# Low parts of 14 weight tiles subtracted on GpSimd, last taps behind q and k, and a reordered head in a one-layer hybrid decoder kernel

## The chip, the cores and the metric

The kernel is one program on one core of a Trainium2 chip. The metric is the device time in microseconds of one execution, as the median of several; less is better. The engines are TensorE (PE, with its weight loads PEld), VectorE (DVE), ScalarE (ACT), GpSimd (POOL) and SyncE (SP, which here only issues DMAs). They run in parallel, each takes its own instructions strictly in program order, and they wait for each other by semaphores.

## The reference

One decoder layer for a sequence of 256 tokens, width 1024, all in float32:

```python
mod = silu(c) @ ada_w + ada_b                      # six vectors of 1024: shift, scale, gate, twice
xn = rmsnorm(x, norm1_g) * (1 + sc1) + sh1
q, k, v, ca, cg = split(xn @ w_in)                 # 5 x 512 columns
y_attn = attention(rmsnorm(q), rmsnorm(k), v)      # 8 heads of 64, causal, with a relative bias table
a = causal_dwconv(ca * sigmoid(cg))                # 31 taps, 512 channels
a = silu(group_norm(a))
x = x + g1 * (concat(y_attn, a) @ w_out)
xn2 = rmsnorm(x, norm2_g) * (1 + sc2) + sh2
u, g = split(causal_dwconv(xn2 @ w_up))            # 3 taps, 2 x 2816 channels
x = x + g2 * ((silu(g) * u) @ w_down)
```

With 256 tokens the attention has one block, so it is plain causal attention.

## The kernel before

**Tiles and the two parts of a number.** All weights arrive as 71 tiles of 128 partitions x 2048 float32 (1 MB each), in the order of the list `STREAM`: 24 `ada` tiles (the modulation), 4 `conv` tiles (the a and gate columns of the convolution), 4 `qk`, 2 `v`, 4 `out`, then `up` and `down` tiles of the feed-forward part in turn. SP issues one DMA per tile into a ring of 6 slots (`RAW`, tile `raw`). It issues tile n only when the tile 6 places ahead has been given up: an ada tile by PE (`ada_used`), another by the engine that subtracts its low part (`lo_done`). `SPLIT` numbers the tiles that aren't ada: conv 0 to 3, qk 4 to 7, v 8 and 9, out 10 to 13, up0 14, up1 15.

A product in nearly full float32 precision is made of three fast ones (`product`, L853 to L855): hi times hi, lo times hi, hi times lo. For each such tile, ACT copies the raw tile to `w_hi` (L336, `split_hi`), rounded, and DVE subtracts that from the raw tile into `w_lo` (L543, `split_lo`). There are 3 buffers (`PARTS`) for each, so tile m waits until PE has used tile m-3 (`w_used`). Activations are split in the same way (`act_hi`, `act_lo`).

**The head.** x arrives transposed in `xt`. ACT squares it (L342), PE sums the squares over partitions with a matrix of ones (L898), ACT takes the root, DVE the reciprocal (`rinv`, L549). For each of 8 tiles k of 128 channels: PE multiplies ada tile k with silu(c) (`ada_rows`, L909), ACT copies the rows (L348), PE turns them into columns (`ada_columns`, L923), DVE makes scale and shift (L565 to L569) and the modulated tile (L593, L596), ACT makes `act_hi` (L363), GpSimd (k under 5, L304) or DVE (L558) makes `act_lo`, and PE multiplies with the first two conv tiles (`first_products`). `PRODUCTS_AFTER` and `HIGH_AFTER` say after which ada tile PE and ACT do which k.

**The middle.** PE works through conv2, conv3 and the four qk tiles (some 7 us each with the ada tile behind it), then v in four halves (`v_half`), the rms of q and k (`qk_turn`, `qk_spread` L1018). DVE meanwhile does the depthwise convolution: 124 `taps` of 128x256 (62 for each of two pairs of channel tiles, L621; they accumulate in PSUM), one L543 for each weight tile, and q's and k's normalisation (`qk_normalise`, L675). In its order, 98 taps come before the reciprocal for q and k (L679), and all remaining 26 before `qk_normalise`.

**Attention, heads 0 to 7.** PE makes the scores (L1096), DVE adds the bias and takes the maximum (`add_bias`, L700), ACT the exponentials (L416), DVE divides (`normalise`, two L713 of 128x128 and 128x256), PE turns the probabilities (`head_turn`, L1106) and multiplies with v (L1116). Between heads PE does remaining ada tiles and the first six of eight parts of the output projection (`out_part`). DVE also makes the group norm's split parts (`mix_parts`, L663 and L666) at head 5, ACT copies the highs of out0 to out3 and up0 behind heads 0, 2, 4, 5, 6 (`HIGH_AT_HEAD`), DVE subtracts their lows behind heads 1, 4, 5, 6, 7 (`LOW_AT_HEAD`). GpSimd squares for the group norm (L309).

**Second norm.** DVE scales the projection by the gate (L767), GpSimd and DVE add the residual (L315, L775), DVE and ACT sum the squares (L777), PE transposes back (L1201), ACT, DVE and GpSimd make the parts of the second activations (L493, L783, L786, L319). The feed-forward part follows: 11 rounds of two up tiles and one down tile.

## Time and profile before

| | |
|---|---|
| median of 3 runs | 377.09 us (376.81 to 379.04) |
| the profiled execution's own time | 377.13 us, of which span 375.3 us |
| PE busy | 352.0 us (94%) |
| DVE busy | 267.4 us (71%) |
| ACT busy | 176.9 us (47%) |
| POOL busy | 23.9 us (6%) |
| DMA | 79.51 MB, mean 212 GB/s |
| mean granted TensorE clock | 0.986 |

"Busy" is the union of an engine's instruction times. All times below are in microseconds from the start of the span; the span begins with the first instruction and ends with the last.

### The profile page before, as it was taken

How to read it: one execution, taken by the hardware profiler on the slowest of the kernel's cores; microseconds unless marked ns; L12 is line 12 of the kernel's file. 1: busy time of each engine (PE TensorE's matmuls, PEld its weight loads, DVE VectorE, ACT ScalarE, POOL GpSimd, SP SyncE). 2: the span in 40 equal slices, each digit the busy share in tenths (PEclk: the TensorE clock that was granted, in tenths of full speed). 3: DMA queues.
4: the chain of work that ended last, by engine and by line, in shares of the span. 5: the costliest groups of instructions: out<-in, count | busy, mean ns of one | idle time of the engine just before them, and what ended most of it. 6: DMA issues, size and time to landing. Idle time of an engine off the chain costs nothing.

```text
span 375.3 us, 6080 instructions
## 1 busy us (share of the span) xinstructions
PE 352.0 (94%) x2408; PEld 295.6 (79%) x2408; DVE 267.4 (71%) x486; ACT 176.9 (47%) x251; POOL 23.9 (6%) x67
## 2 busy tenths in 40 slices
PE   1999899999499989999999999999999999999995
PEld 1677788897245437777799899998989899999984
DVE  0393799999996558756888776768586667658665
ACT  3442833352102465837674553635544644636430
POOL 7421000000000200002300000000000000000000
PEclk9999999999889899999999999999999999999999
DMA  8999958798774496551074544654635545510003
GB/s 317 428 422 417 366 209 329 260 344 346 312 289 160 152 371 261 203 199 47 2 283 167 220 148 194 221 165 176 223 123 217 186 160 215 176 50 2 3 0 113
DMA packets 12653, 79.51 MB, mean 212 GB/s; under 512 B 1352, under 2 KB 2768, under 8 KB 3280
## 3 DMA queue, kind: packets, MB, share of 16 engines
q1 hardware_dynamic: 12416, 78.97, 55.2%
q8 instruction: 19, 0.31, 0.3%
q10 hardware_dynamic: 144, 0.13, 0.1%
q14 instruction: 10, 0.08, 0.1%
q0 software_dynamic: 64, 0.01, 0.0%
HBM read 78.05 MB, written 1.06 MB: 211 GB/s over the span
## 4 chain that ended last, share of the span: by engine, by line
PE 80%; DVE 12%; ACT 3%; DMA 3%; issue 1%; POOL 0%; SPq 0%; DVEq 0%; ACTq 0%; POOLq 0%
PE bank L853 22%; PE bank L854 21%; PE bank L855 21%; DVE bank L621 5%; PE bank L875 4%; DVE w_lo L543 2%; PE bank L898 2%; PE bank L1096 2%; PE bank L909 1%; DMA xt<-in_x_t 1%; DMA raw<-in_stream 1%; PE bank L1116 1%; PE bank L1106 1%; PE bank L1018 1%; ACT w_hi L336 1%
## 5 line engine op out<-in xcount | busy, mean ns | idle before, releaser
L853 PE MATMUL bank<-act_hi,w_hi 128*128 128x256 f32 x480 | 137.8, 287 | 2.7 <-DVE glu L630 1.1
L543 DVE TENSOR_TENSOR w_lo<-raw,w_hi 128x2048 fp32r<-128x2048 f32 x47 | 108.2, 2303 | 42.1 <-ACT w_hi L336 42.0
L854 PE MATMUL bank<-act_lo,w_hi 128*128 128x256 f32 x480 | 135.7, 283 | 0.0
L855 PE MATMUL bank<-act_hi,w_lo 128*128 128x256 f32 x480 | 135.6, 283 | 0.0
L853 PEld LDWEIGHTS bank<-act_hi,w_hi 128*128 128x128 f32 x480 | 91.8, 191 | 9.3 <-issue 4.0
L336 ACT ACTIVATE w_hi<-raw 128x2048 fp32r<-128x2048 f32 x47 | 89.7, 1908 | 15.1 <-DMA raw<-in_stream 14.1
L854 PEld LDWEIGHTS bank<-act_lo,w_hi 128*128 128x128 f32 x480 | 92.0, 192 | 0.4
L855 PEld LDWEIGHTS bank<-act_hi,w_lo 128*128 128x128 f32 x480 | 91.9, 191 | 0.0
L621 DVE SCALAR_TENSOR_TENSOR bank<-glu,cols,bank 128x256 f32<-128x256 f32 x116 | 46.2, 492 | 0.0
L503 ACT ACTIVATE bias<-bank,cols 128x256 f32<-128x256 f32 x44 | 22.3, 557 | 35.7 <-PE bank L855 35.7
L853 PE MATMUL bank<-w_hi,hid_hi 128*128 128x512 f32 x88 | 34.8, 396 | 0.0
L854 PE MATMUL bank<-w_lo,hid_hi 128*128 128x512 f32 x88 | 34.8, 395 | 0.0
L855 PE MATMUL bank<-w_hi,hid_lo 128*128 128x512 f32 x88 | 34.7, 394 | 0.0
L517 ACT ACTIVATE hid_hi<-bias 128x256 fp32r<-128x256 f32 x22 | 9.2, 419 | 49.2 <-DVE bias L808 49.2
L794 DVE SCALAR_TENSOR_TENSOR bias<-bank,cols,bias 128x255 f32<-128x255 f32 x44 | 20.6, 482 | 16.4 <-ACT bias L503 16.0
L853 PE MATMUL bank<-w_hi,act_hi 128*128 128x512 f32 x48 | 19.7, 411 | 0.0
L855 PEld LDWEIGHTS bank<-w_hi,hid_lo 128*128 128x128 f32 x88 | 16.5, 188 | 4.0
L875 PE MATMUL bank<-raw,silu_c 128*32 128x512 f32 x128 | 19.4, 708 | 0.0
L853 PEld LDWEIGHTS bank<-w_hi,hid_hi 128*128 128x128 f32 x88 | 16.6, 188 | 3.5
L854 PEld LDWEIGHTS bank<-w_lo,hid_hi 128*128 128x128 f32 x88 | 16.5, 188 | 3.5
L799 DVE SCALAR_TENSOR_TENSOR bias<-bank,cols,bias 128x254 f32<-128x254 f32 x44 | 19.0, 473 | 0.0
L854 PE MATMUL bank<-w_lo,act_hi 128*128 128x512 f32 x48 | 18.8, 391 | 0.0
(155 smaller groups left out, 337.4 us busy)
## 6 DMA issues: line engine op xcount, KB each, us to landing
raw<-in_stream SPq DMA_DIRECT2D x71, 1024.0 KB, 5.5
xt<-in_x_t SPq DMA_DIRECT2D x1, 1024.0 KB, 4.9
bias<-toeplitz_rows SPq DMA_DIRECT2D x1, 1024.0 KB, 10.5
xr<-in_x_rows SPq DMA_DIRECT2D x1, 1024.0 KB, 9.6
out<-xmod SPq DMA_DIRECT2D x3, 256.0 KB, 2.0
...
```

Of the source, the lines that this page charges most:

```text
L336: nc.scalar.activation(w_hi[:, m % PARTS, :], slot(*SPLIT[m]), ACT.Copy).then_inc(hi_done, 1)
L503: nc.scalar.activation(ug[:, t % 2, g, :], bank[4 + 2 * (t % 2) + g][:, 0:SEQ], ACT.Identity, scale=col("ffn_w", (g * FT + t) * FFN_TAPS + 2),
L517: nc.scalar.activation(hid_hi[:, t % 4, :], hid[:, t % 2, :], ACT.Copy).then_inc(hid_hi_ready, 1)
L543: nc.vector.tensor_tensor(w_lo[:, m % PARTS, :], slot(*SPLIT[m]), w_hi[:, m % PARTS, :].bitcast(f32), ALU.subtract).then_inc(lo_done, 1)
L621: nc.vector.scalar_tensor_tensor(to, glu[:, j, i:i + SEQ], w, conv_sum(j), ALU.mult, ALU.add).then_inc(tap, 1)
L794: nc.vector.scalar_tensor_tensor(ug[:, t % 2, g, 1:], bank[4 + 2 * (t % 2) + g][:, 0:SEQ - 1], col("ffn_w", (g * FT + t) * FFN_TAPS + 1), ...
L799: nc.vector.scalar_tensor_tensor(ug[:, t % 2, g, 2:], bank[4 + 2 * (t % 2) + g][:, 0:SEQ - 2], col("ffn_w", (g * FT + t) * FFN_TAPS), ug[: ...
L853: nc.tensor.matmul(o, sh, mh, start=first, stop=False)
L854: nc.tensor.matmul(o, sh, ml, start=False, stop=False)
L855: return nc.tensor.matmul(o, sl, mh, start=False, stop=last)
L875: last = nc.tensor.matmul(bank[to][32 * q:32 * q + 32, :], silu_c[:, k:k + 1].to_broadcast([P, 32]), slot("ada", n)[:, 512 * q:512 * q + 5 ...
L898: last = nc.tensor.matmul(bank[7][:, 0:SEQ], ones[:, :], xmod[:, k, :], start=(k == 0), stop=(k == KT - 1))
```

## The change

1. `POOL_LOW` lists the split tiles 2 to 15 (conv2, conv3, qk, v, out, up0, up1). DVE's `split_lo` returns at once for them, and GpSimd does them: 8 ahead of its two group norm squares, 5 behind these, and up1 behind its two residual additions and ahead of its four `act_lo`. `low_done` lets PE and SP wait for the engine that did a tile. DVE keeps 33 of its 47 subtractions of 128x2048.
2. On DVE, 6 taps instead of 22 lie between the copy of q's and k's rms and the first `qk_normalise`; 16 taps come behind the last one, and ahead of `add_bias(0)`.
3. The head: x is fetched first, in two halves; ACT squares the left half, DVE the right one. ACT's table for the root is loaded by a dummy ahead of its use. 8 dummy products of `ones` stand at PE's start. The stream has conv0 ahead of ada1. Of conv0 and conv1 the high and low parts are made in a quarter (512 columns) and the rest. PE's order is a hand-written list with products of one conv tile at a time up to k = 2. GpSimd fills the bias rows in three portions between its `act_lo` tiles.

```diff
-PRODUCTS_AFTER = {3: (0,), 4: (1, 2), 5: (3,), 6: (4,), 7: (5,), 8: (6, 7)}
-HIGH_AFTER = {2: (0,), 3: (1, 2), 4: (3,), 5: (4,), 6: (5,), 7: (6,), 8: (7,)}
-STREAM = [("ada", 0), ("ada", 1), ("conv", 0), ("ada", 2), ("conv", 1),
+STREAM = [("ada", 0), ("conv", 0), ("ada", 1), ("ada", 2), ("conv", 1),
+POOL_LOW = list(range(2, SP_AT["up", 1] + 1))
+PIECE = SLOT // 4
...
+        def low_done(eng, m):
+            by_dve, by_pool = lows_through(m)
+            if m in POOL_LOW:
+                eng.wait_ge(lo_pool_done, by_pool)
+            else:
+                eng.wait_ge(lo_done, by_dve)
-        LOW_AT_HEAD = {1: SP_AT["out", 0], 4: SP_AT["out", 1], 5: SP_AT["out", 2], 6: SP_AT["out", 3], 7: SP_AT["up", 0]}
...
+            sp.dma_start(xt[:, 0:KT // 2, :], x_t[:, 0:KT // 2, :]).then_inc(xt_left, 16)
+            sp.dma_start(xt[:, KT // 2:, :], x_t[:, KT // 2:, :]).then_inc(xt_right, 16)
             sp.dma_start(cols[:, :], cols_in).then_inc(cols_ready, 16)
-            sp.dma_start(xt[:, :, :], x_t).then_inc(xt_ready, 16)
...
             for k in range(POOL_LOWS):
+                if 1 <= k <= 3:
+                    fill_rows(buckets[9 * (k - 1):9 * k])
...
+            def split_lo(m):
+                pool.wait_ge(hi_done, m + 1)
+                arrived(pool, *SPLIT[m])
+                if m >= PARTS:
+                    pool.wait_ge(w_used, m - PARTS + 1)
+                nc.gpsimd.tensor_tensor(w_lo[:, m % PARTS, :], slot(*SPLIT[m]),
+                                        w_hi[:, m % PARTS, :].bitcast(f32), ALU.subtract).then_inc(lo_pool_done, 1)
...
-            split_hi(0)
-            copy_rows(0)
-            act.wait_ge(consts_ready, 1)
             act.wait_ge(ssq_ready, 1)
...
+            copy_rows(0)
+            split_hi_first(0)
+            for k in range(KT):
+                if k == 3:
+                    split_hi_first(1)
+                if k >= 1:
                     copy_rows(k)
+                if k == KT - 1:
                     split_hi(FIRST)
+                xn_high(k)
...
-            taps(len(TAPS))
+            taps(6)
             qk_normalise(0)
             qk_normalise(1)
...
             qk_normalise(3)
+            taps(len(TAPS))
...
-            for k in range(KT):
-                ada_rows(k)
-                if k >= 1:
-                    ada_columns(k - 1)
-                if k == 2:
-                    keep_clock(30, 3)
-                for tile in PRODUCTS_AFTER.get(k, ()):
-                    first_products(tile)
-            ada_columns(KT - 1)
-            for tile in PRODUCTS_AFTER[KT]:
-                first_products(tile)
+            ada_rows(0)
+            ada_columns(0)
+            keep_clock(16, 5)
+            ada_rows(1)
+            first_products(0, (0,))
...
+            ada_columns(4)
+            for k in range(5, KT):
+                ada_rows(k)
+                first_products(k - 2)
+                ada_columns(k)
+            first_products(KT - 2)
+            first_products(KT - 1)
```

GpSimd's instructions from its residual additions on, before the change:

```order
L309 TENSOR_TENSOR xmod<-conv 128x512 [waits gn_centred] x2
L315 TENSOR_TENSOR xr<-xr,qk 128x512 [waits x2_part,xr_ready]
L315 TENSOR_TENSOR xr<-xr,qk 128x512 [waits x2_part]
L319 TENSOR_TENSOR act_lo<-xt,act_hi 128x256 [waits xn2_hi] x4
L324 TENSOR_TENSOR xmod<-xr,qk 128x256 [waits out_part]
```

and the same stretch of the changed kernel:

```order
L349 TENSOR_TENSOR xmod<-conv 128x512 [waits gn_centred] x2
L340 TENSOR_TENSOR w_lo<-raw,w_hi 128x2048 [waits w_used,raw_ready4,hi_done]
L340 TENSOR_TENSOR w_lo<-raw,w_hi 128x2048 [waits w_used,raw_ready5,hi_done]
L340 TENSOR_TENSOR w_lo<-raw,w_hi 128x2048 [waits w_used,raw_ready0,hi_done]
L340 TENSOR_TENSOR w_lo<-raw,w_hi 128x2048 [waits w_used,raw_ready1,hi_done]
L340 TENSOR_TENSOR w_lo<-raw,w_hi 128x2048 [waits w_used,raw_ready2,hi_done]
L359 TENSOR_TENSOR xr<-xr,qk 128x512 [waits x2_part,xr_ready]
L359 TENSOR_TENSOR xr<-xr,qk 128x512 [waits x2_part]
L340 TENSOR_TENSOR w_lo<-raw,w_hi 128x2048 [waits w_used,raw_ready3,hi_done]
L365 TENSOR_TENSOR act_lo<-xt,act_hi 128x256 [waits xn2_hi] x4
```

Five subtractions (out0 to out3, up0) now stand between the squares and the residual additions, with no wait that ties them to DVE, and up1's stands right behind the second addition.

On DVE, the stretch from the last loop taps to the first head's bias, before the change (`bank<-glu` is a tap, `qk<-qk` a normalisation):

```order
L543 TENSOR_TENSOR w_lo<-raw,w_hi 128x2048 [waits w_used,raw_ready0,hi_done]
L621 SCALAR_TENSOR_TENSOR bank<-glu,cols,bank 128x256 [waits tap] x28
L679 RECIPROCAL qk_inv<-qk_stat 128x32 [waits qk_std]
L621 SCALAR_TENSOR_TENSOR bank<-glu,cols,bank 128x256 [waits tap] x4
L682 COPY qk_rstd<-bank 16x256 [waits qk_turned]
L621 SCALAR_TENSOR_TENSOR bank<-glu,cols,bank 128x256 [waits tap] x20
L621 SCALAR_TENSOR_TENSOR conv<-glu,cols,bank 128x256 [waits tap] x2
L675 SCALAR_TENSOR_TENSOR qk<-qk,q_gain,bank 128x256 [waits qk_raw,qk_bc]
```

and of the changed kernel:

```order
L684 SCALAR_TENSOR_TENSOR bank<-glu,cols,bank 128x256 [waits tap] x34
L742 RECIPROCAL qk_inv<-qk_stat 128x32 [waits qk_std]
L684 SCALAR_TENSOR_TENSOR bank<-glu,cols,bank 128x256 [waits tap] x4
L745 COPY qk_rstd<-bank 16x256 [waits qk_turned]
L684 SCALAR_TENSOR_TENSOR bank<-glu,cols,bank 128x256 [waits tap] x6
L738 SCALAR_TENSOR_TENSOR qk<-qk,q_gain,bank 128x256 [waits qk_raw,qk_bc]
...
L738 SCALAR_TENSOR_TENSOR qk<-qk,cols,bank 128x256
L684 SCALAR_TENSOR_TENSOR bank<-glu,cols,bank 128x256 [waits tap] x14
L684 SCALAR_TENSOR_TENSOR conv<-glu,cols,bank 128x256 [waits tap] x2
L764 ISA prob,peak<-bank,bias 128x128 [waits scores,bias_ready]
```

The weight tile's subtraction is gone, and the last 16 taps stand behind the normalisations, right ahead of the first head.

At the end of ACT's head (`act_hi<-xt` is the modulated tile's high part, `w_hi<-raw` conv2's), the changed kernel has, as before, conv2's copy ahead of the last activation tile:

```order
L397 ACTIVATE mod_rows<-bank 128x256 [waits norm1_turned,ada_used]
L407 ACTIVATE act_hi<-xt,shift,scale 128x256 [waits norm1_scale,xhat_ready]
L397 ACTIVATE mod_rows<-bank 128x256 [waits norm1_turned,ada_used]
L382 ACTIVATE w_hi<-raw 128x2048 [waits raw_ready4]
L407 ACTIVATE act_hi<-xt,shift,scale 128x256 [waits norm1_scale,xhat_ready]
L432 ACT_TABLE_LOAD
```

What moved is who waits for it: the copy now releases a subtraction on GpSimd instead of one on DVE behind DVE's last `act_lo`.

## Rows read from the trace of the kernel before

**Rows 1.** Busy time by stage: stretch, length, busy us by engine, clock, DMA share, GB/s.

```profile
24.00:27.00 3.00, 2.69 (x29) 1.77 (x28) 2.92 (x7) 0.94 (x2) 1.12 (x1) 1.00 1.01 423
...
45.00:75.00 30.00, 29.92 (x243) 26.18 (x244) 29.43 (x53) 11.19 (x12) 0.00 (x0) 1.00 0.70 261
```

**Rows 2.** PE in order of time, middle: start, us, line, tiles, [idle before, releaser].

```profile
96.22 0.39 PE L855 MATMUL bank<-w_hi,act_lo 128*128 128x512 f32 x1
101.98 0.59 PE L994 MATMUL bank<-ident,qk_inv 128*16 128x128 f32 x2 [5.37 <-DVE qk_inv L679]
...
107.52 1.99 PE L1018 MATMUL bank<-qk_rstd,from_group 16*128 16x256 f32 x8
112.40 1.06 PE L875 MATMUL bank<-raw,silu_c 128*32 128x512 f32 x8
...
118.30 0.93 PE L1096 MATMUL bank<-qk 64*128 64x128 f32 x8
...
122.08 0.55 PE L1106 MATMUL bank<-ident,prob 128*128 128x128 f32 x3 [0.93 <-DVE prob L713]
```

**Rows 3.** DVE in order of time, the taps that PE waits for there.

```profile
90.60 11.07 DVE L621 SCALAR_TENSOR_TENSOR bank<-glu,cols,bank 128x256 f32<-128x256 f32 x28
```

**Rows 4.** A cost group of the page: shape, count, busy us, mean ns, idle before.

```profile
L543 DVE TENSOR_TENSOR w_lo<-raw,w_hi 128x2048 fp32r<-128x2048 f32 x47 | 108.2, 2303 | 42.1 <-ACT w_hi L336 42.0
```

**Rows 5.** POOL and DVE beside each other, in order of time, at three places.

```profile
24.48 1.12 POOL L304 TENSOR_TENSOR act_lo<-xmod,act_hi 128x256 fp32r<-128x256 f32 x1 [2.14 <-ACT act_hi L363]
24.92 0.96 DVE L593 TENSOR_TENSOR xt<-xt,rinv 128x256 f32<-128x256 f32 x1
27.05 0.73 POOL L304 TENSOR_TENSOR act_lo<-xmod,act_hi 128x256 fp32r<-128x256 f32 x1 [1.45 <-ACT act_hi L363]
...
123.70 1.04 POOL L309 TENSOR_TENSOR xmod<-conv 128x512 f32<-128x512 f32 x1
123.75 1.14 DVE L713 TENSOR_SCALAR prob<-prob,rtotal 128x256 f32<-128x256 f32 x1
...
172.38 1.30 POOL L315 TENSOR_TENSOR xr<-xr,qk 128x512 f32<-128x512 f32 x1 [47.64 <-DVE qk L767]
172.89 1.33 DVE L775 TENSOR_TENSOR xr<-xr,qk 128x512 f32<-128x512 f32 x1
174.21 1.38 DVE L767 TENSOR_TENSOR qk<-bank,gate 128x512 f32<-128x512 f32 x2
174.98 1.27 POOL L315 TENSOR_TENSOR xr<-xr,qk 128x512 f32<-128x512 f32 x1 [1.30 <-DVE qk L767]
176.25 0.68 DVE L775 TENSOR_TENSOR xr<-xr,qk 128x512 f32<-128x512 f32 x1
176.97 0.69 DVE L777 CUSTOM_DVE_ANT_0 xmod<-xr 128x512 f32<-128x512 f32 x1
```

**Rows 6.** ACT, DVE and PE in order of time, around the copies for out1 to out3.

```profile
136.67 1.90 ACT L336 ACTIVATE w_hi<-raw 128x2048 fp32r<-128x2048 f32 x1
138.59 0.55 DVE L713 TENSOR_SCALAR prob<-prob,rtotal 128x128 f32<-128x128 f32 x2
140.56 0.55 PE L1106 MATMUL bank<-ident,prob 128*128 128x128 f32 x3
...
151.08 1.91 ACT L336 ACTIVATE w_hi<-raw 128x2048 fp32r<-128x2048 f32 x1
155.57 1.90 ACT L336 ACTIVATE w_hi<-raw 128x2048 fp32r<-128x2048 f32 x1
158.30 0.55 PE L1106 MATMUL bank<-ident,prob 128*128 128x128 f32 x3
```

**Rows 7.** ACT and PE in order of time in the head.

```profile
13.59 1.91 ACT L336 ACTIVATE w_hi<-raw 128x2048 fp32r<-128x2048 f32 x1 [5.55 <-DMA raw<-in_stream]
...
36.62 1.07 PE L909 MATMUL bank<-raw,silu_c 128*32 128x256 f32 x16
...
45.08 0.36 PE L853 MATMUL bank<-act_hi,w_hi 128*128 128x256 f32 x1 [1.05 <-DVE glu L630]
```

More of the change, by code:

```diff
@@ L56, with lows_through @@
 RAW, PARTS = 6, 3
+POOL_LOW = list(range(2, SP_AT["up", 1] + 1))
+def lows_through(m):
+    on_pool = sum(p <= m for p in POOL_LOW)
+    return m + 1 - on_pool, on_pool
+PIECE = SLOT // 4
 COLS = {}
@@ L864, in ready @@
             def ready(m):
-                pe.wait_ge(lo_done, m + 1)
+                low_done(pe, m)
                 pe.wait_ge(hi_done, m + 1)
@@ L893, in keep_clock @@
                     nc.tensor.transpose(bank[to][:, 0:P], ident[:, :], ident[:, :])
-            pe.wait_ge(consts_ready, 1)
-            pe.wait_ge(xsq_ready, 1)
+            pe.wait_ge(ones_ready, 1)
+            for _ in range(8):
+                nc.tensor.matmul(bank[3][:, 0:P], ones[:, :], ones[:, :], start=True, stop=True)
             for k in range(KT):
+                pe.wait_ge(xsq_left if k < KT // 2 else xsq_right, 1)
                 last = nc.tensor.matmul(bank[7][:, 0:SEQ], ones[:, :], xmod[:, k, :], start=(k == 0), stop=(k == KT - 1))
@@ L925, in ada_columns, with first_products @@
                 last.then_inc(norm1_turned, 1)
-            def first_products(k):
+            def first_products(k, tiles=range(FIRST)):
                 pe.wait_ge(xn_hi, k + 1)
@@ L933, in first_products @@
                     pe.wait_ge(xn_lo, k - POOL_LOWS + 1)
-                for m in range(FIRST):
+                for m in tiles:
                     if k == 0:
+                        pe.wait_ge(lo_piece, m + 1)
+                        pe.wait_ge(hi_piece, m + 1)
+                    elif k == 2:
                         ready(m)
```

104 lines of the change are left out of this document (68 added, 36 removed).

## The prediction

> **What bounds the kernel now.** I read the stages first: busy time by stretch, to find where PE isn't full. From 45 to 75 PE is busy 29.92 of 30 us [rows 1]; there a faster DVE buys nothing. Then PE's order of time, for its waits: the one large hole lies at 96.61 (the end of the v product, 96.22 + 0.39) to 101.98, 5.37 us, and the releaser is DVE's reciprocal for q and k [rows 2]. DVE in the same stretch is inside 28 taps, 11.07 us or 0.395 each [rows 3]: it is late because it is full, with taps and with one subtraction of 2.30 us per weight tile [rows 4]. Behind the hole PE is slow as well: from 102.57 to 107.52 it does three ada tiles, 4.95 us, where one takes 1.06 at 112.40 [rows 2]; 1.7 us are lost to a lower clock. Last, since the change is about two engines side by side, I read POOL and DVE against each other in order of time [rows 5].
>
> **What a moved subtraction costs.** POOL has no 128x2048 in this trace. Its two-tile operation takes 0.73 for 256 columns and 1.27 to 1.30 for 512 [rows 5]: 0.56 for 256 more, so 0.73 + 7 x 0.56 = 4.65 us. Bounds: eight times the smallest, 5.8, above; below, the slope to the squares' 1.04 [rows 5], 0.73 + 7 x 0.31 = 2.9. I take 4.65, since L304 and L315 read two tiles as this one does, and the squares read one twice. Against PE's pace this hides: conv and qk tiles take PE some 7 us each, two buffers ahead, and even 5.8 is under 7.
>
> **What it does to DVE.** An operation on one engine holds the other up. L775 reads two tiles in SBUF: 0.68 alone, 1.33 when it begins inside POOL's L315 (172.38 to 173.68), that is, it runs when L315 ends. L713 of 256 columns, one tile in SBUF at double rate, took 1.14 beside L309; the pair of L713 takes 0.55 elsewhere [rows 5, 6]. It works the other way too, and the one that waits comes next: L304 at 24.48 took 1.12 instead of 0.73, behind DVE, and L593, due at 24.92, then came after it, 0.96 long [rows 5]. But L767, which reads PSUM and one SBUF tile, took 0.69 each, twice, across the start of L315 at 174.98 [rows 5]. So taps (one SBUF tile, one PSUM bank) shouldn't be held up, while `act_lo`, the division of the probabilities, `mix_parts`, the residual sum and its squares are, each for up to the whole 4.65. The Trainium skill says the same more generally ("SBUF — State Buffer", "Who interferes with whom"): VectorE and GpSimd share a port pair as an exclusive lock, which takes in a two-input VectorE operation in SBUF against a GpSimd one that reads it, and whoever is second waits for the whole instruction. It speaks against this change wherever DVE is on the path; by it the holds below are full length, without it the sum is that of rival 1.
>
> **Head.** DMA runs without a hole at 423 GB/s [rows 1], a tile per 1048.6 / 423 = 2.48 us; conv0, third in the stream, is there at 13.59 [rows 7]. So conv2 (eleventh) arrives at 13.59 + 8 x 2.48 = 33.4 whatever the order. The early work (x first, squares halved on two engines, PE warm, table loaded) brings rinv some 8 us forward, but PE then needs 1.07 for ada rows, some 0.6 for columns and 12 products (1.4) a tile, 3.1 us, against 2.48 from DMA, and POOL's fills and the split pieces stand in front of the early products. Tile 2's `act_lo` I place at 21.8 (ada2 is there at 16.1, then rows, columns, scale, GpSimd's fills and its turns with DVE's pieces; an estimate to 1 us). Behind it PE has 0.7 of product, five ada rows (5.0 without their pipeline's end), three products with one conv tile (2.1), four columns (2.2) and two full products (2.8): ada 7's rows are done at 34.6 to 34.8, against 37.69 before (36.62 + 1.07) [rows 7]. Then: copy of rows and conv2's high part on ACT, +2.45; POOL starts conv2's low part at once, +2.5 to +7.15; the last activation tile's `act_lo` on DVE, due at +3.1, is held up until +7.15; product, sigmoid and glu follow, 2.2 us, so conv2 starts at +9.35 = 44.1. Before it was 45.08 [rows 7]. Gain 0.9; bounds: 2.8 gained if PE keeps up with DMA, 1.5 lost if the hold catches the scale of k = 7, due only 0.2 us ahead of POOL's start.
>
> **Middle.** PE is full until the v product, so the gain of the head stays. DVE loses eight subtractions, 8 x 2.30 = 18.4 us, and is ready long before the product ends: the hole of 5.37 goes, and with it the 1.7 of clock. In before's times PE turns at 96.6 and would have the scores at 118.30 - 5.37 - 1.7 = 111.2. But 16 taps now stand between the last normalisation and the first bias. Before, the spreads ended at 115.45 (112.40 + 1.06 + 1.99) and two DVE operations followed, to 116.3; now 109.2, and 16 x 0.395 = 6.3 more: 115.5. The first head's bias waits for that. Before, PE turned head 0 at 122.08, 2.85 after the scores' end (118.30 + 0.93); now about 2.7 after 115.5, at 118.2. Gain 3.9, not 7; what is late next is the tail of the taps.
>
> **Attention.** DVE gets rid of four of its lows here (9.2 us) but it wasn't the bound; PE is. POOL gets out0 to up0 as soon as ACT has copied each. In before's times [rows 6]:
> - out1: its copy ends at 138.57, POOL begins at 138.6, between the two L713 of head 3 (138.59 and 138.8). If it catches the second, that ends at 143.6 instead of 139.1, and PE's turn at 140.56 waits 3.1 us. The margin is 0.15 us; I count it.
> - out2 and out3: the copies end at 152.99 and 157.47. POOL is busy from 153.1 or 153.4 to 158.0 and again to 162.7. DVE has the last of `mix_parts` there and head 6's two L713, ready from 156. One operation gets in between POOL's two, the next one waits: head 6 is normalised at 163.3, and its turn, 158.30 before, waits 5.0 us.
>
> **Second norm.** Here DVE is the path: L775 at 176.25, L777 at 176.97 [rows 5], then root, diagonal and transposes. POOL's up1 starts at the end of its own L315, 176.25, its wait long fulfilled. Whichever of the two it meets waits for 4.65: loss 4.4 (bounds 2.6 and 5.6 by the bounds of the operation). up1's low part was covered before by up0's products.
>
> **Sum.** -0.9 - 3.9 + 3.1 + 5.0 + 4.4 = +7.7. The profiled execution took 377.13, 0.04 above the median of 377.09: 384.8. The feed-forward part is full of PE and moves as a whole. The new holes of 3 to 5 us may lower PE's clock as the one of 5.37 did; that is 0 to 2 us each and not in the sum, but in the range.
>
> **Rivals.**
> 1. The holds don't bite: POOL's long operation lets DVE in, or its starts fall beside the path. For it: out1's margin is 0.15 us, and no row shows a hold longer than 0.8 us. Against it: four rows, at three places, all full length. Then -0.9 - 3.9 = -4.8: 372.3, faster. It decides where holds on the path sum to less than 1 us.
> 2. Only the second norm bites, since there POOL and DVE are released by the same event, while in attention shifts of a few tenths help: -4.8 + 4.4 = -0.4, 376.7. With out1's as well, 379.8; both are no change.
> 3. The taps are held up too. They take two inputs and a pointer. Then each of eight subtractions costs DVE 4.65 - 2.30 more, 18.8 us, less the 5.3 that DVE stands idle now around the spreads: hole of 19 instead of 5.4 before q and k, some 395 and more with the rest. L767's undisturbed pair speaks against it.
> 4. GpSimd's order delays a tile that PE waits for. Up to 4.65 + 1.9 a tile against 7 us of PE, it can't in the middle; up1's low part is done at 181, while PE first has the whole of up0 to do. No time of its own.
>
> **How the numbers follow.** The holds in attention and the second norm together (one or both in attention): 0.50, 380 to 390. Rival 2 with at most out1: 0.25, 375 to 380. Rival 1: 0.20, 369 to 374. Rival 3: 0.05. A tenth lies above 390 (clock, rival 3) and under a tenth below 371.5; so 371.5 to 390, and 380 to 390 for the likeliest alone. A change of this kernel is told from none at about 1%, 3.8 us. Faster by more: rival 1 and a luckier head, 0.23. Slower by more, above 380.9: most of the likeliest and rival 3, 0.50. Within: 0.27.
>
> **What would show it.** In the changed profile: POOL's 128x2048 near 4.65 us, less where nothing contends. PE without its 5.4 us hole before the q and k turn, but with a wait of some 2 us and again 1.5 before head 0's turn, released by the taps. Conv2's first product near 44. L775 or L777 with a duration near 5 us at the second norm, one L713 near 4.8 at head 3 and one at head 6, with PE's turn behind them. If these last three have their old 0.3 to 0.7, rival 1 is right and the time is near 372. A tap of more than 0.5 us beside POOL would be rival 3. The forecast is wrong altogether if the head gains much more than 3 us, which DMA's rate seems to exclude.

## The result, and the profile after

| | before | after |
|---|---|---|
| median | 377.50 us (376.81 to 379.04) | 399.13 us (394.87 to 402.23) |
| profiled execution, span | 377.13, 375.3 us | 397.09, 395.3 us |
| PE, DVE, POOL busy | 352.0, 267.4, 23.9 us | 361.8, 260.4, 90.3 us |
| mean granted clock | 0.986 | 0.961 |

The changed kernel is slower: its time is 1.046 of the time before, 95% interval 1.039 to 1.053. The ratio goes by two of its four executions, 394.87 and 397.09; the other two (401.18 and 402.23) lie over 1.5% above the lowest and are left out of it. The 377.50 of the kernel before has one execution more than the table ahead of the prediction. The forecast was 384.8, slower, with a range up to 390. The direction was right, the time lies above the range: the two profiled executions differ by 20.0 us where the sum gave 7.7.

The page of the kernel after: the granted clock over 40 slices (each 9.9 us), then the costs of the two engines that subtract low parts, and of the taps:

```profile
PEclk9999899999996888789989999999999999999999
...
L592 DVE TENSOR_TENSOR w_lo<-raw,w_hi 128x2048 fp32r<-128x2048 f32 x31 | 71.4, 2304 | 23.8 <-ACT w_hi L382 23.7
L340 POOL TENSOR_TENSOR w_lo<-raw,w_hi 128x2048 fp32r<-128x2048 f32 x14 | 64.0, 4583 | 62.1 <-ACT w_hi L382 62.1
L684 DVE SCALAR_TENSOR_TENSOR bank<-glu,cols,bank 128x256 f32<-128x256 f32 x116 | 46.0, 480 | 0.0
```

DVE's 47 instructions of [rows 4] are 33 now, 31 of them of full width. GpSimd needs 4.58 for one, near the 4.65 of the forecast. The taps did not get longer (480 ns, 492 before).

Two words are used from here on. A hold is the time for which a DVE instruction stands because a GpSimd instruction is running. A head's turn is the start of the transposes of its probabilities on PE (`head_turn`).

Four places carry the loss. **Head**, GpSimd, DVE and PE in order of time:

```profile
37.96 4.52 POOL L340 TENSOR_TENSOR w_lo<-raw,w_hi 128x2048 fp32r<-128x2048 f32 x1 [6.76 <-ACT w_hi L382]
...
38.41 4.23 DVE L657 TENSOR_SCALAR xmod<-xt,scale,shift 128x256 f32<-128x256 f32 x1 [0.34 <-DVE scale L630]
42.67 0.42 DVE L619 TENSOR_TENSOR act_lo<-xmod,act_hi 128x256 fp32r<-128x256 f32 x1
...
34.56 1.07 PE L971 MATMUL bank<-raw,silu_c 128*32 128x256 f32 x16
...
43.24 0.36 PE L913 MATMUL bank<-act_hi,w_hi 128*128 128x256 f32 x1 [4.10 <-DVE act_lo L619]
...
45.28 0.55 PE L913 MATMUL bank<-act_hi,w_hi 128*128 128x256 f32 x1
```

conv2's low part begins on GpSimd at 37.96. The modulation of the last activation tile (L657; its seven others take 0.41 each) comes 0.45 later and takes 4.23: it ends 0.16 behind GpSimd's instruction. PE stands for 4.10, and conv2's first product starts at 45.28, where it started at 45.08 before [rows 7].

**The q and k stage and head 0**, DVE and PE:

```profile
109.88 5.58 DVE L684 SCALAR_TENSOR_TENSOR bank<-glu,cols,bank 128x256 f32<-128x256 f32 x14
115.37 0.86 DVE L684 SCALAR_TENSOR_TENSOR conv<-glu,cols,bank 128x256 f32<-128x256 f32 x2
116.15 0.28 DVE L764 CUSTOM_DVE_ANT_0 prob<-bank,bias 128x128 f32<-128x128 f32 x1
...
97.64 0.38 PE L1072 MATMUL bank<-ident,qk_inv 128*16 128x128 f32 x2
...
116.38 1.10 PE L1104 MATMUL bank<-conv,half_mean 128*128 128x256 f32 x4 [2.42 <-DVE conv L684]
118.85 0.65 PE L1184 MATMUL bank<-ident,prob 128*128 128x128 f32 x3 [1.37 <-DVE prob L777]
...
134.42 0.55 PE L1184 MATMUL bank<-ident,prob 128*128 128x128 f32 x3
```

The wait of 5.37 ahead of the q and k turn [rows 2] is gone. The 16 taps behind the normalisations take its place in part: PE waits 2.42 and 1.37, and head 0's turn comes at 118.85 instead of 122.08 [rows 2]. But head 2's turn (134.42) comes no sooner than before, at 134.41. The two stretches from head 0's turn to head 2's, as busy times by stage (columns as in [rows 1]), after:

```profile
118.85:134.42 15.57, 15.57 (x72) 6.33 (x72) 4.89 (x14) 5.96 (x12) 6.56 (x3) 0.67 0.50 176
```

and before:

```profile
122.08:134.41 12.33, 12.33 (x72) 5.72 (x72) 7.00 (x15) 5.99 (x12) 2.04 (x2) 0.86 0.54 194
```

PE has the same 72 matmuls and is busy all the time in both. In PE's own columns only the clock and with it the times differ, 0.67 and 0.86. That takes back the 3.2 us won.

**Heads 3 to 6**, GpSimd, DVE and PE:

```profile
138.65 4.59 POOL L340 TENSOR_TENSOR w_lo<-raw,w_hi 128x2048 fp32r<-128x2048 f32 x1 [12.23 <-ACT w_hi L382]
157.59 9.07 POOL L340 TENSOR_TENSOR w_lo<-raw,w_hi 128x2048 fp32r<-128x2048 f32 x2 [14.35 <-ACT w_hi L382]
...
138.60 4.79 DVE L777 TENSOR_SCALAR prob<-prob,rtotal 128x128 f32<-128x128 f32 x2
157.45 9.56 DVE L726 CAST act_hi<-xmod 128x256 fp32r<-128x256 f32 x4
166.93 1.42 DVE L729 TENSOR_TENSOR act_lo<-xmod,act_hi 128x256 fp32r<-128x256 f32 x4
...
143.45 0.90 PE L1184 MATMUL bank<-ident,prob 128*128 128x128 f32 x3 [2.81 <-DVE prob L777]
167.49 0.77 PE L913 MATMUL bank<-w_hi,act_hi 128*128 128x512 f32 x1 [7.59 <-DVE act_lo L729]
```

At 138.60 the pair of divisions takes 4.79, not the 0.55 of [rows 6]. At 157.45 the four casts of the group norm's part take 9.56: they start 0.14 ahead of two subtractions that stand back to back. PE waits 7.59 for the parts behind them. Before the change the casts were

```profile
151.56 0.90 DVE L663 CAST act_hi<-xmod 128x256 fp32r<-128x256 f32 x4
```

**Second norm**, where the operations of the end of [rows 5] stand now:

```profile
191.32 4.52 POOL L340 TENSOR_TENSOR w_lo<-raw,w_hi 128x2048 fp32r<-128x2048 f32 x1
...
189.32 1.38 DVE L829 TENSOR_TENSOR qk<-bank,gate 128x512 f32<-128x512 f32 x2
191.37 5.01 DVE L837 TENSOR_TENSOR xr<-xr,qk 128x512 f32<-128x512 f32 x1
...
198.07 3.47 PE L1279 MATMUL bank<-diag,xr 128*128 128x128 f32 x16 [4.39 <-DVE diag L823]
```

The last residual sum takes 5.01 instead of 0.68.

By PE's order of time (before and after: the start of conv2's products, their end, the heads' turns) the 20.0 us divide like this: head +1.2, of which 1.0 in conv2's products, middle -4.4, clock from head 0 to head 2 +3.2, out1's hold +2.9, heads 3 to 5 +3.0, out2 and out3 +9.2, second norm +4.9. The time of the turn of each head, in several profiles, us (one execution each):

| head | 0 | 2 | 3 | 4 | 5 | 6 | 7 |
|---|---|---|---|---|---|---|---|
| before | 122.08 | 134.41 | 140.56 | 145.80 | 150.70 | 158.30 | 165.05 |
| after | 118.85 | 134.42 | 143.45 | 150.34 | 156.59 | 173.39 | 180.16 |
| e1_out_up_on_dve | 121.20 | 136.79 | 142.94 | 148.18 | 153.07 | 160.67 | 167.43 |
| e2_conv2_too | 117.14 | 130.79 | 136.94 | 143.80 | 150.27 | 157.87 | 164.62 |
| e10_after_clock_kept | 121.15 | 133.48 | 142.51 | 149.31 | 155.71 | 172.59 | 179.34 |
| e12_clock_kept_head3 | 118.56 | 129.24 | 137.95 | 143.67 | 149.59 | 167.78 | 174.55 |

### The profile page after: what moved, and what is told of

Same layout as the page of the kernel before. It is cut to its first block, busy times and chain, and to the rows that moved or that the text cites. A ratio compares the mean times of both kernels' runs of the same rounds, so it can differ in the third digit from the quotient of the medians.

```text
span 395.3 us, 6095 instructions
## 1 busy us (share of the span) xinstructions
PE 361.8 (92%) x2410; PEld 303.4 (77%) x2410; DVE 260.4 (66%) x475; ACT 176.2 (45%) x255; POOL 90.3 (23%) x81
## 4 chain that ended last, share of the span: by engine, by line
PE 82%; DVE 13%; ACT 2%; issue 1%; DMA 1%; POOL 0%; ACTq 0%; DVEq 0%; POOLq 0%
PE bank L913 23%; PE bank L914 22%; PE bank L915 22%; PE bank L935 5%; DVE act_hi L726 2%; PE bank L960 1%; DVE bank L684 1%; DVE prob L777 1%; PE bank L971 1%; DVE xr L837 1%; PE bank L1194 1%; PE bank L1174 1%; PE bank L1184 1%; DVE xmod L657 1%; DMA xt<-in_x_t 1%
## 5 line engine op out<-in xcount | busy, mean ns | idle before, releaser
L915 PE MATMUL bank<-act_hi,w_lo 128*128 128x256 f32 x480 | 136.3, 284 | 0.0
L382 ACT ACTIVATE w_hi<-raw 128x2048 fp32r<-128x2048 f32 x45 | 85.8, 1907 | 7.8 <-DMA raw<-in_stream 6.7
L592 DVE TENSOR_TENSOR w_lo<-raw,w_hi 128x2048 fp32r<-128x2048 f32 x31 | 71.4, 2304 | 23.8 <-ACT w_hi L382 23.7
L340 POOL TENSOR_TENSOR w_lo<-raw,w_hi 128x2048 fp32r<-128x2048 f32 x14 | 64.0, 4583 | 62.1 <-ACT w_hi L382 62.1
L913 PE MATMUL bank<-w_hi,hid_hi 128*128 128x512 f32 x88 | 34.8, 396 | 0.0
L914 PE MATMUL bank<-w_lo,hid_hi 128*128 128x512 f32 x88 | 34.8, 395 | 0.0
L913 PE MATMUL bank<-w_hi,act_hi 128*128 128x512 f32 x48 | 20.9, 436 | 7.6 <-DVE act_lo L729 7.6
L914 PE MATMUL bank<-w_lo,act_hi 128*128 128x512 f32 x48 | 19.8, 412 | 0.0
L915 PE MATMUL bank<-w_hi,act_lo 128*128 128x512 f32 x48 | 19.5, 407 | 0.0
```

The lines of the kernel that those rows point to most:

```text
L340: nc.gpsimd.tensor_tensor(w_lo[:, m % PARTS, :], slot(*SPLIT[m]), w_hi[:, m % PARTS, :].bitcast(f32), ALU.subtract).then_inc(lo_pool_done, 1)
L382: nc.scalar.activation(w_hi[:, m % PARTS, :], slot(*SPLIT[m]), ACT.Copy).then_inc(hi_done, 1)
L592: nc.vector.tensor_tensor(w_lo[:, m % PARTS, :], slot(*SPLIT[m]), w_hi[:, m % PARTS, :].bitcast(f32), ALU.subtract).then_inc(lo_done, 1)
L913: nc.tensor.matmul(o, sh, mh, start=first, stop=False)
L914: nc.tensor.matmul(o, sh, ml, start=False, stop=False)
L915: return nc.tensor.matmul(o, sl, mh, start=False, stop=last)
```

## Experiments

Ratios are to the kernel before on the same chip, with 95% intervals. The median of the kernel before was 376.98 to 379.88 on these chips, so times of runs on different chips compare only to some 3 us: e1 to e4 share one chip, e5 to e8 another, e9 to e11 a third, e12 has its own. Theory A: the loss is GpSimd's long subtractions holding DVE. Theory B: it is the reordered head or the taps. A third question came up with the table above: what the clock does.

### Which subtractions cost what

**e1_out_up_on_dve.** The low parts of out0 to out3, up0 and up1 back on DVE, where they stood before; all else as changed. The edit is shown against the changed kernel.

```diff
-POOL_LOW = list(range(2, SP_AT["up", 1] + 1))
+POOL_LOW = list(range(2, SP_AT["v", 1] + 1))
...
+                if h in LOW_AT_HEAD:
+                    split_lo(LOW_AT_HEAD[h])
...
+            split_lo(SP_AT["up", 1])
```

> The changed kernel with the low parts of out0 to out3, up0 and up1 back on VectorE, at the places they had before; conv2 to v1 stay on GpSimd. Theory A (a GpSimd subtraction of 4.6 us holds up any VectorE operation on the path that reads two SBUF tiles or copies inside SBUF, and the slower clock behind the waits adds to it): the three holds of the changed profile go (2.9 us at head 3, 9.2 at mix_parts, 4.9 at the second norm, some 3 of clock between them), so 395.3 - 20 = about 375 us of span, 377 us of time, level with the kernel before. Rival B (GpSimd's work in the conv and qk stage is what costs, by ring or taps): above 385 us.

378.78 us, ratio 0.9987 (0.995 to 1.002). From head 2's turn to head 7's it takes 30.64, exactly as before (the table), where the changed kernel takes 45.74. Behind head 2's turn 20.0 us come back with these six tiles; the two profiled spans differ by 17.6 (395.3 and 377.7), because e1's head took 2.4 longer (its clock was 0.5 from 22.5 to 25.9 and from 43.0 to 49.8, that of the changed kernel from 44.1 to 47.5). What is left of the change is worth nothing together.

**e2_conv2_too.** e1 with conv2's low part on DVE as well: GpSimd keeps conv3, qk and v.

```diff
-POOL_LOW = list(range(2, SP_AT["v", 1] + 1))
+POOL_LOW = list(range(3, SP_AT["v", 1] + 1))
```

> As the run with out and up on VectorE, and conv2's low part on VectorE as well (GpSimd has conv3, qk and v, 7 tiles). Theory A: the modulated tile of k = 7 was held 3.8 us (4.23 instead of 0.42) at the end of the head by conv2's subtraction; without it conv2 starts near 42 us instead of 46 to 47, so 3 to 4 us less than the run before it: 373 us, and faster than the kernel before by about 1%. Rival: the head is bound by TensorE's own list or by DMA, then no more than 1 us is gained, 376.

374.91 us, ratio 0.989 (0.983 to 0.995): faster than before by about 1%. PE in order of time:

```profile
44.56 0.35 PE L919 MATMUL bank<-act_hi,w_hi 128*128 128x256 f32 x1 [0.87 <-DVE glu L695]
...
114.67 1.10 PE L1110 MATMUL bank<-conv,half_mean 128*128 128x256 f32 x4 [2.41 <-DVE conv L686]
```

The wait of 4.10 is gone. conv2 starts at 44.56 here. In the other profiles of the same head it starts at 42.08 to 42.29 (e3, e7, e8), 43.22 (e11) and 44.21 (e9). In the three late ones the clock was 0.5 for 3.4 us (e11) or 6.8 us (e2, e9) between 20 and 28, in the three early ones it was not; what decides that is open. So up to 2.5 us of a time here can be this.

**e4_before_up1_only.** The kernel before, with nothing but up1's low part moved to GpSimd behind its second residual addition.

```diff
+POOL_LOW = [SP_AT["up", 1]]
...
+            if SP_AT["up", 1] in POOL_LOW:
+                split_lo(SP_AT["up", 1])
```

> The kernel before with one edit: up1's low part on GpSimd, behind its second residual addition. Theory A: the residual sum or its squares on VectorE take near 5.0 us instead of 0.68, and the time is 377.1 + 4.4 = 381.5 us, up to 383 with a slower clock behind. Rival C (a hold of full length needs the other changes, or the wait is made good by up0 and up1 being ready): 377 to 378 us.

383.74 us, ratio 1.012 (1.008 to 1.016). DVE and PE:

```profile
178.62 5.01 DVE L807 TENSOR_TENSOR xr<-xr,qk 128x512 f32<-128x512 f32 x1
...
185.32 1.01 PE L1233 MATMUL bank<-diag,xr 128*128 128x128 f32 x3 [4.39 <-DVE diag L793]
```

One moved instruction, a loss of 1.2%, or 4.1 us against the 379.68 that the kernel before took on this chip (the expectation started from 377.1), with the same 5.01 as in the changed kernel.

**e5_pieces_of_512.** The changed kernel with each of GpSimd's low parts in four instructions of 512 columns.

```diff
-                nc.gpsimd.tensor_tensor(w_lo[:, m % PARTS, :], slot(*SPLIT[m]),
-                                        w_hi[:, m % PARTS, :].bitcast(f32), ALU.subtract).then_inc(lo_pool_done, 1)
+                for a in range(0, SLOT, PIECE):
+                    last = nc.gpsimd.tensor_tensor(w_lo[:, m % PARTS, a:a + PIECE], slot(*SPLIT[m])[:, a:a + PIECE],
+                                                   w_hi[:, m % PARTS, a:a + PIECE].bitcast(f32), ALU.subtract)
+                last.then_inc(lo_pool_done, 1)
```

> The changed kernel with each of GpSimd's 14 subtractions cut into four of 512 columns, 1.28 us each: more GpSimd work in all (5.1 us a tile instead of 4.6), but no single instruction over 1.3 us. Theory A (a VectorE operation waits for the GpSimd instruction that runs, not for all of GpSimd's queue): head 3's division waits at most 1.2 us and TensorE not at all; at mix_parts each of the first five operations waits for one piece, so TensorE waits some 4.5 us instead of 7.6; second norm 2 to 2.5 instead of 4.4; end of the head 2 to 3 less. In all 382 to 386 us. Rival (VectorE is held for as long as GpSimd has work queued): 397 or more.

385.11 us (two executions), ratio 1.016 (1.008 to 1.024). GpSimd, DVE and PE at heads 3 and 5:

```profile
136.53 5.09 POOL L341 TENSOR_TENSOR w_lo<-raw,w_hi 128x512 fp32r<-128x512 f32 x4 [11.55 <-ACT w_hi L384]
...
136.48 1.56 DVE L779 TENSOR_SCALAR prob<-prob,rtotal 128x128 f32<-128x128 f32 x2
...
138.45 0.55 PE L1186 MATMUL bank<-ident,prob 128*128 128x128 f32 x3
157.37 0.47 PE L915 MATMUL bank<-w_hi,act_hi 128*128 128x512 f32 x1 [3.25 <-DVE act_lo L731]
```

The pair takes 1.56 instead of 4.79 and PE no longer waits at head 3; at head 5 it waits 3.25 instead of 7.59. At the second norm it waits 2.39 instead of 4.39, at the end of the head 1.80 instead of 4.10. The same work in shorter instructions gives back 12.4 us of the profiled span (395.3 and 382.9), by the ratios some 11: a hold lasts as long as the one instruction that runs, and DVE comes in between two.

**e6_memset_for_out_up.** For out0 to up1 GpSimd writes zeros into `w_lo` and reads nothing. The low parts of these six tiles are left out.

```diff
+                if m > SP_AT["v", 1]:
+                    nc.gpsimd.memset(w_lo[:, m % PARTS, :].bitcast(f32), 0.0).then_inc(lo_pool_done, 1)
+                    return
```

> The changed kernel with GpSimd's subtractions for out0 to out3, up0 and up1 replaced by a fill of the same tile with zero, at the same place and under the same waits: GpSimd writes SBUF and reads nothing (the low parts of these six weight tiles are left out of the result). If only the read side is shared: the residual sum (two SBUF inputs) takes its 0.68 us at the second norm, and mix_parts' casts their 0.29. If the whole port pair is locked by any GpSimd instruction: all of them are held for the length of the fill (some 1.8 us by the fill of 1024 columns in 0.94). If reading and writing are separate locks: casts and divisions (which use both sides twice) are held by the fill, the two-input operations are not. Time 383 to 389 us in each case, since the fill is shorter.

381.38 us (one execution), below the expected 383 to 389. GpSimd and DVE at heads 3 and 5 and at the second norm:

```profile
141.30 1.81 POOL L341 MEMSET w_lo<- 128x2048 f32 x1 [14.91 <-ACT w_hi L385]
155.84 1.81 POOL L341 MEMSET w_lo<- 128x2048 f32 x1 [12.74 <-ACT w_hi L385]
179.00 1.81 POOL L341 MEMSET w_lo<- 128x2048 f32 x1
...
141.27 2.05 DVE L780 TENSOR_SCALAR prob<-prob,rtotal 128x128 f32<-128x128 f32 x2
155.18 1.43 DVE L732 TENSOR_TENSOR act_lo<-xmod,act_hi 128x256 fp32r<-128x256 f32 x4
178.76 2.12 DVE L826 TENSOR_SCALAR diag<-ident,rinv 128x128 f32<-128x128 f32 x1
179.07 1.82 DVE L840 TENSOR_TENSOR xr<-xr,qk 128x512 f32<-128x512 f32 x1
```

The two TENSOR_SCALAR instructions end with the memset (2.05 and 2.12 instead of 0.55 and 0.39), the four subtractions of two SBUF tiles at 155.18 run on through the memset that begins at 155.84, at their usual 1.43. The casts were over before it, so this run says nothing on them. The residual sum ends with the TENSOR_SCALAR ahead of it, so whether it was held itself can't be told. The Trainium skill ("SBUF — State Buffer", "Who interferes with whom") says the same: copies, casts and TENSOR_SCALAR, in their modes with two ports, contend with GpSimd, a two-input operation only with a GpSimd instruction that reads SBUF. The trace agrees for TENSOR_SCALAR (2.05 and 2.12 under a write) and for the two-input operation (1.43 under a write, while the residual sum took 5.01 under a subtraction that reads).

### The taps' order, and GpSimd in the middle

**e3_no_gpsimd_low.** New head and new order of the taps, every low part on DVE. The edit is shown against e2.

```diff
-POOL_LOW = list(range(3, SP_AT["v", 1] + 1))
+POOL_LOW = []
```

> The new head and the new order of the last taps alone: no low part of a weight tile on GpSimd. Theory A: conv2 starts near 42 us, TensorE has its hole before the turn of q and k again since VectorE is full, but the q and k normalisation no longer waits for the last taps: 373 to 375 us. If the seven tiles on GpSimd are worth their 16 us of VectorE time on the path, this run is slower than the one with conv2 on VectorE by 1 us or more; if the 5 us gained there are given back to the tail of the taps and the clock, both are level.

386.22 us, ratio 1.019 (1.015 to 1.023), a miss by 11 us or more. PE:

```profile
100.58 0.60 PE L1078 MATMUL bank<-ident,qk_inv 128*16 128x128 f32 x2 [5.80 <-DVE qk_inv L744]
121.37 1.16 PE L1110 MATMUL bank<-conv,half_mean 128*128 128x256 f32 x4 [2.41 <-DVE conv L686]
```

The head alone is good (conv2 at 42.08, 3.0 sooner than before). But without GpSimd's seven tiles the wait ahead of the q and k turn is back, and the tail of taps costs its own on top. The expectation had taken the tail for free. Compared with the kernel before, 3.2 us are lost between the q and k turn and head 0's, and 7.1 from there to head 5's turn, where the clock was 0.5 for 18.9 us instead of 3.4. Against e2, GpSimd's subtractions of conv3, qk and v are worth 11.3 us (same chip): there DVE does taps and GpSimd's work beside them holds up little.

**e11_old_tap_order.** e2, with the 16 taps back ahead of the normalisation.

```diff
-            taps(6)
+            taps(len(TAPS))
             qk_normalise(0)
...
             qk_normalise(3)
-            taps(len(TAPS))
```

> e2_conv2_too with the taps in the order of the kernel before: 22 of them between the copy of q's and k's rms and the first normalisation, none behind the last one. The new head and GpSimd's seven subtractions (conv3, qk, v) stay. Theory: with GpSimd doing these, DVE stands idle for 1.56 and 3.52 us between the normalisations, and the 16 taps behind them only delay head 0. Here the four normalisations end at about 109.5 (96.7 + 22 x 0.40 = 105.5, and 4 more), the scores come at 110.3 as before, and head 0's turn at about 114.1 instead of 117.14; PE waits for no group norm mean, and the clock behind it stays up longer as well. So 3 to 5 below e2's 374.9: 370 to 372. Rival, the changed order of the taps was right by itself and the old one delays the scores: 375 to 378.

371.91 us, ratio 0.984 (0.978 to 0.990). From the q and k turn to head 0's turn it takes 20.55 (21.21 in e2), and from head 0's to head 2's 10.68 instead of 13.65, at a granted clock of 1.00.

In these stages of the two profiles part 2 of the change loses time once GpSimd has the low parts: 0.7 directly, 3.0 through the clock. The whole times don't show it by themselves: the intervals of e11 and e2 overlap, and the kernel before was 2.7 us faster on e11's chip.

**e8_taps_in_gaps.** e2, with three of the 16 trailing taps ahead of the first normalisation and eight in DVE's gap between q and k; five stay behind the last one.

```diff
-            taps(6)
+            taps(9)
             qk_normalise(0)
...
+            taps(8)
             qk_normalise(2)
             qk_normalise(3)
             taps(len(TAPS))
```

> The same version with the last taps laid into VectorE's two waits for the spreads: 9 (not 6) ahead of the first normalisation, 8 between the second and third, 5 (not 16) behind the last. The tail ahead of the first head's bias shrinks from 6.3 to 2.0 us, so the bias starts when the scores are there: head 0's turn 3 us earlier, TensorE's wait of 2.4 us gone: 371 to 372 us. Rival: the time goes on in later ada tiles that wait for DMA or for a slow clock: under 1 us gained, 374 us.

369.30 us, ratio 0.974 (0.969 to 0.980). Head 0's turn comes 18.12 after the q and k turn, and PE waits 0.93 for it. Yet the clock from head 0 to head 2 is no better than in e2 (0.76, and 0.77 there): 14.02 us. The profiled spans of e8 and e2 differ by 8.3: 3.1 lie between the q and k turn and head 0's and are the edit's, 2.4 lie in the head (q and k turn at 93.52 and 95.93) and 3.2 in heads 3 to 5, which had no stretch at 0.5 here.

### The clock

**e7_clock_kept.** e2 with 18 and 10 transposes of `ident` in PE's two waits ahead of head 0's turn; nobody reads them.

```diff
             pe.wait_ge(v_ready, ST)
+            pe.wait_ge(mod_rows_ready, 1)
+            keep_clock(18, 2)
             gn_means(1)
+            keep_clock(10, 2)
```

> The version with conv3, qk and v alone on GpSimd (374.9 us measured), and 18 and 10 transposes of the identity put into TensorE's two waits ahead of head 0's turn (2.4 and 1.4 us). Theory: the clock at 0.5 for 6.8 us right behind these waits costs some 3 us in heads 0 and 1; with TensorE busy there it stays at full and head 2's turn comes 2 to 3 us earlier: 372 us. Rival: these ada tiles wait for DMA, not for the clock: no gain, 375 us.

370.50 us, ratio 0.976 (0.969 to 0.984): 4.4 less than e2. Head 2's turn comes 12.33 after head 0's (13.65 in e2), head 5's 16.29 after head 2's (19.48 in e2). Only the first of these, 1.3, is where the transposes are meant to act; heads 3 to 5 run in 16.28 in e1 as well, with no transposes, so those 3.2 can't be credited to the edit.

**e9_taps_and_clock.** e8 with 4 and 6 such transposes.

```diff
+            pe.wait_ge(mod_rows_ready, 1)
+            keep_clock(4, 2)
             gn_means(1)
+            keep_clock(6, 2)
```

> e8_taps_in_gaps with 4 and 6 identity transposes ahead of and behind the second group norm mean's products, so that PE has no pause around head 0's turn. In e8 the clock was 0.5 at 113.69 to 117.10 and 120.51 to 123.93 and head 2's turn came 14.02 after head 0's (12.33 in the kernel before, 15.57 in the changed one). If these two stretches follow PE's short pauses at heads 0 and 1: head 2's turn comes about 12.5 to 13 after head 0's, and the time is 1 to 1.5 below e8's 369.3: 367.5 to 368.5. Rival, the clock falls for what PE did earlier (small products in the q and k stage), or the added transposes cost as much as they save: 369 to 370.

366.85 us (365.03 to 371.27), ratio 0.968 (0.960 to 0.977), the lowest of all; the interval overlaps e8's, and the kernel before was 2.9 us faster on this chip than on e8's. Head 2's turn comes 10.67 after head 0's, 3.35 sooner than in e8:

```profile
113.72:124.39 10.67, 10.67 (x74) 5.53 (x72) 6.99 (x15) 5.96 (x12) 2.04 (x2) 1.00 0.65 220
```

That is more than expected; in this profile the head was 2.1 later (q and k turn at 95.59, in e8 at 93.52) and hides a part of it.

**e10_after_clock_kept.** The changed kernel with e7's 18 and 10 transposes and nothing else.

> The changed kernel with nothing but 18 and 10 identity transposes put into PE's two waits (2.42 and 1.37 us) ahead of head 0's turn. All low parts stay where the change put them. Theory: these two waits lower the clock at 119.16 to 132.8 and that costs 3.2 us by head 2's turn (134.42); without it head 2's turn is at 131.0 to 131.8, while head 3's normalisation is still held by out1's subtraction (PE waits 2.5 to 3). If the lost clock also is what moved the group norm's casts into GpSimd's two subtractions of out2 and out3, they may come free of them again and PE's wait there be nearer to 5 than to 7.6. So 3.2 to 6 below 399.1: 393 to 396. Rival, the clock doesn't hang on these waits: head 2's turn stays at 134 and the time at 398 to 400.

395.75 us, ratio 1.048 (1.041 to 1.054; the kernel before had 376.98 here). From head 0's turn to head 2's it takes 12.33 instead of 15.57, so the expected 3.2 came in that stage. In the whole time it does not show: the four executions (394.73 to 397.65) lie where 394.87 and 397.09 of the changed kernel do. The profiled one was slower in the head, with a clock of 0.5 for 10.2 us there instead of 3.4, so that head 0's turn came 2.3 later. The casts were not freed:

```profile
156.56 9.22 POOL L340 TENSOR_TENSOR w_lo<-raw,w_hi 128x2048 fp32r<-128x2048 f32 x2 [14.26 <-ACT w_hi L382]
...
156.57 9.56 DVE L726 CAST act_hi<-xmod 128x256 fp32r<-128x256 f32 x4
...
166.61 0.77 PE L913 MATMUL bank<-w_hi,act_hi 128*128 128x512 f32 x1 [7.62 <-DVE act_lo L729]
```

Head 5's turn still comes 6.40 after head 4's, 4.90 before.

**e12_clock_kept_head3.** e10 with 23 more in PE's wait at head 3.

```diff
+                if h == 3:
+                    pe.wait_ge(mod_rows_ready, 2)
+                    keep_clock(23, 5)
                 head_turn(h)
```

> e10_after_clock_kept with 23 more identity transposes in PE's wait at head 3, which out1's subtraction causes. In e10 this wait is followed by a clock of 0.5 at 142.35 to 145.77 and 149.18 to 152.59, head 4's and head 5's turns come 6.80 and 6.40 after the turn before (5.24 and 4.90 in the kernel before), and the group norm's casts then begin 0.07 after ACT's copy of out2 has ended, right under GpSimd's subtraction (9.56 us for four casts, PE waits 7.62). In the kernel before they began 1.43 ahead of that copy's end. Theory: the half clock is the reason for both. With it gone, the turns of heads 3 to 5 are 5.3 and 4.9 apart, the four casts take about 0.9 again, and the hold falls on the split parts behind them and on head 6's pair; PE waits for 4.5 to 6 there. So 3.1 to 5.7 below e10's 395.75: 390 to 392.7. Rival, the casts' place under the subtraction doesn't hang on the clock: four casts of 9 us and PE's wait of 7.6 stay, and only some 3 us are won.

389.74 us, ratio 1.027 (1.019 to 1.035). The time is just below what was expected, but not by that mechanism. GpSimd, DVE and PE:

```profile
133.85 4.53 POOL L340 TENSOR_TENSOR w_lo<-raw,w_hi 128x2048 fp32r<-128x2048 f32 x1 [7.83 <-ACT w_hi L382]
150.92 9.15 POOL L340 TENSOR_TENSOR w_lo<-raw,w_hi 128x2048 fp32r<-128x2048 f32 x2 [12.54 <-ACT w_hi L382]
...
133.42 0.55 DVE L777 TENSOR_SCALAR prob<-prob,rtotal 128x128 f32<-128x128 f32 x2
136.17 2.23 DVE L767 TENSOR_SCALAR npeak<-peak 128x2 f32<-128x2 f32 x1
150.45 5.27 DVE L726 CAST act_hi<-xmod 128x256 fp32r<-128x256 f32 x4
155.65 5.71 DVE L729 TENSOR_TENSOR act_lo<-xmod,act_hi 128x256 fp32r<-128x256 f32 x4
...
135.38 2.73 PE L953 MATMUL bank<-ident 128*128 128x128 f32 x23
160.50 0.77 PE L913 MATMUL bank<-w_hi,act_hi 128*128 128x512 f32 x1 [7.58 <-DVE act_lo L729]
```

Here out1's subtraction missed the pair (133.42, over before 133.85) and held a TENSOR_SCALAR of two columns instead (136.17, 2.23 instead of 0.17), which cost PE little: the forecast's margin of some tenths, seen from its other side. So there was no wait for the 23 transposes to fill: they took 2.73 us of PE's own time, head 3's turn came 8.71 after head 2's (9.03 in e10, 6.15 before), and the clock was 0.5 from 142.5 to 145.9 all the same. The casts begin 0.47 ahead of GpSimd now and some of them get through, and PE still waits 7.58, because it waits for the parts behind them, and those end behind the second subtraction either way. The rival was right on the wait. Against e10's profile (span 389.7 and 394.4) 2.6 of the 4.7 us are there at head 0's turn already, that is in the head, whose clock the edit does not touch; 1.65 lie between the turns of heads 0 and 2. From head 2's turn to head 7's, where the edit acts, only 0.55 are won (45.31 and 45.86).

## Why the prediction was right in sign and too low

**The hold, right.** All four places that it named had their hold, two of them on a neighbour of the operation named: L777 at head 3, the group norm's casts instead of head 6's pair, L837 at the second norm, the last tile's modulation instead of its `act_lo` in the head. e4 and e5 show the mechanism by itself. The taps and the gate product (L829, 1.38 for two, as before) were not held, so rival 3 is out: 480 ns a tap. Rivals 1 and 2 are out by these holds and by e1. Rival 4 cost no time: POOL has 0% of the chain that ended last.

**Head: -0.9 forecast, +1.2.** Two slips. ada 7's rows ended at 35.6, not at 34.8. And the step read "the last activation tile's `act_lo`" as what is held; in fact it was the modulation ahead of it (L657), so `act_lo` came 0.4 behind the hold's end. That gives 44.1 + 0.8 + 0.4 = 45.3, as measured. The other 1.0 is clock: 0.5 right behind PE's wait of 4.10, so that conv2's products took 6.90 instead of 5.92. In all six profiled kernels with conv2 on GpSimd (the changed one, e1, e5, e6, e10, e12) the clock falls at 41.7 to 44.1, in none of the other eight. e2 shows that conv2's tile on GpSimd turned a gain of up to 3 us into this loss.

**Middle: -3.9 forecast, -4.4.** Right, step by step: the hole closed, the tail of 16 taps next, add_bias at 116.15 where 115.5 was forecast and the head had shifted by 1.2. What was missing is what the two waits behind it cost in clock.

**out1: +3.1 forecast, +2.9.** Right in profile and size; that it was hit at a margin of 0.15 us was also luck, since in e12 the pair came 0.43 ahead of GpSimd and was not held. (The prediction says that DVE gets rid of four of its lows in attention; there are five, out0 to up0. No term hangs on it.)

**out2 and out3: +5.0 forecast, +9.2.** The term was mis-sized, and the place was off. It took the casts at 151.56 and most of the parts as done when GpSimd begins 1.5 later, and let head 6's pair take the hold. That 1.5 hangs on head 5's turn coming 4.90 after head 4's, since DVE's casts follow PE's scores and ACT's copy of out2 does not. The interval was 6.25 after, 6.40 in e10 and 5.92 in e12; 1.5 less the excess gives 0.15, 0.0 and 0.48, and the trace has 0.14, -0.01 and 0.47 between the casts' and GpSimd's start. With less than 1.5, two subtractions of 4.6 stand in front of parts that PE needs: a wait of 7.6, not 5.0. In e10 and e12 the excess is itself clock (0.5 from 149.2 to 152.6 and from 142.5 to 145.9), as it is in the changed kernel (149.9 to 153.3); no run shows the place with 1.5 left. Another 1.6 is clock behind the wait (0.5 from 163.5 to 170.4).

**Second norm: +4.4 forecast, +4.9.** Right; the 0.5 is clock.

**The steps that failed.** They are two: the clock, which was put at nothing in the sum, and the hold of out2 and out3, sized at 5.0 where PE waited 7.6. For the clock, the prediction gave new holes "0 to 2 us each and not in the sum, but in the range". Summed over the places it was 3.2 (heads 0 to 2), 3.0 (heads 3 to 5), 1.6, 1.0 and 0.5: 9.3 of the 12.3 us that the sum lacked; the rest is 2.6 of hold and 1.1 of head, less 0.7 in the middle and at head 3. It counted as holes only those of 3 to 5 us. The costliest loss followed two short ones, 2.42 and 1.37, that the prediction itself had worked out. A term that cost time at each of five places should have stood in the sum.

That the first 3.2 hang on PE being idle there is borne out by all the profiles together, one execution each. From head 0's turn to head 2's, us:

| taps behind the normalisations, transposes in PE's waits | |
|---|---|
| 16, none (changed, e1, e2, e3, e5, e6) | 15.57, 15.59, 13.65, 14.76, 15.56, 15.81 |
| 16, 18 and 10 (e7, e10, e12) | 12.33, 12.33, 10.68 |
| 5, none (e8) | 14.02 |
| 5, 4 and 6 (e9) | 10.67 |
| none, none (before, e4, e11) | 12.33, 10.68, 10.68 |

For heads 3 to 5 a cause is not shown: e2 and e4 have a clock of 0.5 in that stretch with no hold ahead of it (e4 from 136.3 to 143.1), e1 has 1.0, though e1 and e2 have the same instructions there in the same order. So part or all of those 3.0 may be the chance of one execution; the spread of the changed kernel (394.87 to 402.23) is three times that of the kernel before.
